# A planner for the order of one kernel's work: dense units beyond the heads' share, a fourth output tile, and banks released by their readers alone

## The reference

```
# layer "a": sparse attention; each query keeps its k_top best keys, RoPE on q and k
p = jax.nn.softmax(logits, axis=-1)
o = jnp.einsum('bhqk,bqkhd->bqhd', p, vs)            # 16 heads of 64
x = layer_norm(ALPHA * x + (o * jax.nn.silu(g)) @ w_out, ...)
# layer "b": stick-breaking attention
log_one_minus = jnp.where(before, jax.nn.log_sigmoid(-z), 0.0)
log_stick = lax.cumsum(log_one_minus, axis=3, reverse=True) - log_one_minus
a = jnp.where(before, jnp.exp(jax.nn.log_sigmoid(z) + log_stick), 0.0)
x = layer_norm(ALPHA * x + (o * jax.nn.silu(g)) @ w_out, ...)
```

## Time and profile before

| | us |
|---|---|
| median of 3 runs (1566.52 to 1567.36) | 1566.93 |
| the profiled execution | 1563.4 |
| its span, first to last instruction | 1561.6 |
| PE busy in it | 1524.5 (98%) |
| DVE, ACT, POOL busy | 1159.1, 883.7, 767.4 |
| mean granted TensorE clock | 0.995 of full |

### The profile page before, as it was taken

The page is one execution under the profiler, slowest core; times in us unless marked ns, Lnnn a source line. Parts: engine busy times, 40 slices in busy tenths (PEclk is TensorE's granted clock), DMA queues, the critical chain, the costliest instruction groups (busy, mean ns, idle before and its releaser), DMA issues.

```text
span 1561.6 us, 21827 instructions
## 1 busy us (share of the span) xinstructions
PE 1524.5 (98%) x7798; PEld 1298.5 (83%) x7798; DVE 1159.1 (74%) x2045; ACT 883.7 (57%) x1544; POOL 767.4 (49%) x745
## 2 busy tenths in 40 slices
PE   9999999999999999999999999999999999999987
PEld 7888899988788888888888788887788888888877
DVE  5999989999654688448628469976766828798876
ACT  6444788886433344234324373788884437677743
POOL 2332334434464465455545653466655336667553
PEclk9999999999999999999999999999999999999999
DMA  5988565664332232322222378755468764455551
GB/s 199 215 188 191 139 159 142 155 143 115 122 108 95 81 108 95 98 101 100 95 94 86 116 188 177 177 122 121 96 136 192 174 135 109 108 116 116 119 122 55
DMA packets 60300, 203.28 MB, mean 130 GB/s; under 512 B 6816, under 2 KB 9376, under 8 KB 60192
## 3 DMA queue, kind: packets, MB, share of 16 engines
q1 hardware_dynamic: 41184, 132.66, 25.8%
q0 software_dynamic: 19008, 69.21, 25.7%
HBM read 199.75 MB, written 2.10 MB: 129 GB/s over the span
## 4 chain that ended last, share of the span: by engine, by line
PE 84%; DVE 9%; ACT 5%; issue 1%; DMA 1%; POOL 0%; SPq 0%; ACTq 0%; DVEq 0%
PE bank L364 81%; PE bank L370 2%; DVE r L403 1%; DVE ext L403 1%; DVE r L391 1%; DVE sp_lo L391 1%; ACT soft L374 1%; DVE pt_lo L391 1%; DMA w_lo<-in_weights 0%; ACT w_hi L374 0%; DVE q_both L403 0%; DVE small L403 0%; ACT k_both L374 0%; ACT prob L374 0%; ACT ext L374 0%
## 5 line engine op out<-in xcount | busy, mean ns | idle before, releaser
L410 POOL TENSOR_TENSOR w_lo<-w_raw,w_hi 128x512 fp32r<-128x512 f32 (+1 forms) x187 | 267.8, 1454 | 254.7 <-ACT w_hi L374 254.7
L374 ACT ACTIVATE w_hi<-w_raw 128x1024 fp32r<-128x1024 f32 (+2 forms) x206 | 213.8, 1041 | 282.3 <-PE bank L364 259.8
L364 PE MATMUL bank<-x_hi,w_hi 128*128 128x512 f32 x872 | 346.9, 398 | 4.1 <-DVE q_both L403 1.7
L364 PE MATMUL bank<-x_hi,w_lo 128*128 128x512 f32 x872 | 340.7, 391 | 1.3 <-POOL w_lo L410 1.2
L364 PE MATMUL bank<-x_lo,w_hi 128*128 128x512 f32 x872 | 340.4, 390 | 0.0
L364 PEld LDWEIGHTS bank<-x_hi,w_hi 128*128 128x128 f32 x872 | 164.3, 188 | 36.7 <-ACT k_both L374 2.1
L364 PEld LDWEIGHTS bank<-x_hi,w_lo 128*128 128x128 f32 x872 | 163.8, 188 | 37.2 <-POOL w_lo L410 1.6
L364 PEld LDWEIGHTS bank<-x_lo,w_hi 128*128 128x128 f32 x872 | 164.4, 188 | 30.1
L613 POOL DMA_DIRECT2D w_lo<-in_weights x132 | 117.7, 895 | 135.0 <-ACT w_lo L374 113.8
L364 PE MATMUL bank<-a_hi,w_hi 128*128 128x512 f32 x416 | 162.0, 389 | 0.0
L364 PE MATMUL bank<-a_hi,w_lo 128*128 128x512 f32 x416 | 161.8, 389 | 0.0
(11 more groups left out here) (234 smaller groups left out, 3432.5 us busy)
## 6 DMA issues: line engine op xcount, KB each, us to landing
w_raw<-in_weights SPq DMA_DIRECT2D x223, 512.0 KB, 3.4
w_lo<-in_weights POOLq DMA_DIRECT2D x132, 512.0 KB, 6.8
alibi<-in_alibi SPq DMA_DIRECT2D x16, 256.0 KB, 4.5
w_raw<-in_weights SPq DMA_DIRECT2D x8, 384.0 KB, 3.0
r<-in_x SPq DMA_DIRECT2D x8, 256.0 KB, 6.3
r<-in_x SPq DMA_DIRECT2D x4, 512.0 KB, 6.3
out_y<-r SPq DMA_DIRECT2D x16, 128.0 KB, 1.8
w_raw<-in_weights SPq DMA_DIRECT2D x4, 256.0 KB, 5.6
```

Source lines behind the costliest of these rows:

```text
L364: return e.matmul(out, lhsT, rhs, start=start, stop=stop, skip_group_check=resumed)
L374: return self.act.run(lambda e: e.activation(out, in_, func, **kw), after, 0.07 + size(out) * 0.00086 + 0.09 * len(kw))
L410: return self.pool.run(lambda e: e.tensor_tensor(out, a, b, op), after, cost)
```

## The change

There are five edits.
- `weave`: if no stream of the heads is ripe within FAR = 1.0 us of PE's planned time, a dense unit may be filled in even beyond the share.
- `tiles`: in the heads' phase a dense tile begins only if a bank of its ring is free by plan, either at PE's planned time or at the time at which the next stream is ripe (`until`); otherwise `fill` reports "idle" and the loop goes on to the next stream.
- `stacked` returns besides its results the list of those that read the bank, and the bank is released by these alone (the two copies from `k_both` to `k_both` no longer count).
- `stick_gate`: ACT reads the bank first and releases it; DVE then takes its minimum from the copy in SBUF.
- out_b: a fourth output tile is begun in the heads' phase, after the last weighing (`last_head(1)`), on bank 4 of the ring 0 to 4; `project_and_norm` begins one tile later.

```diff
@@ -41,6 +41,7 @@
 SEAMS = (("kiwi", 0), ("qi", 0), ("vb", 0))
 FIRST_HALVED = {"out_a": 4, "out_b": 4}
 LATE_GATES = 2
+FAR = 1.0
 EXP_AND_TANH = 0
 EXP_AND_LN = 6
 
...
@@ -456,6 +459,10 @@
                 self.pe.wait(b.free)
                 return b
             self.pop()
+
+    def bank_time(self):
+
+        return min([through(b.free) for b in self.ring if not b.open and not b.pending], default=math.inf)
 
     def bank_soon(self):
 
...
@@ -640,6 +647,8 @@
 
         for key in keys:
             while key[0] in ("qa", "ka", "qb", "kb") and key[1] >= 2 and 2 * key[1] - 3 not in self.s_done:
+                yield "idle"
+            while self.in_heads and self.bank_time() > max(self.pe.time, self.until):
                 yield "idle"
             c = self.take(key)
             b = self.bank()
...
@@ -675,8 +684,8 @@
                     used[k] = [tok]
                 self.tick()
                 yield
-        for key in late:
-            while not may():
+        for n, key in enumerate(late):
+            while not may(n):
                 if self.in_heads:
                     yield "idle"
                 else:
...
@@ -885,15 +894,15 @@
         by = [scale if isinstance(scale, float) else scale[r, :] for r in own]
         func = ACT.Copy if isinstance(scale, float) else ACT.Identity
         his = [self.a_op(tiles[a][own[a], :], src[own[a], :], func, ready, scale=by[a]) for a in range(2)]
-        toks = list(his)
+        toks, reads = list(his), list(his)
         if low is not None:
             toks += [self.a_op(tiles[a][own[1 - a], :], tiles[a][own[a], :].bitcast(F32), ACT.Copy, [his[a]]) for a in range(2)]
         for a in range(2):
             yield [his[a]]
             hi = tiles[a][own[a], :]
             lo = tiles[a][own[1 - a], :] if low is None else low[a][own[a], :]
-            toks.append(self.v_stt(lo, src[own[a], :], by[a], hi.bitcast(F32), ALU.mult, ALU.subtract, ready + [his[a]]))
-        return toks
+            reads.append(self.v_stt(lo, src[own[a], :], by[a], hi.bitcast(F32), ALU.mult, ALU.subtract, ready + [his[a]]))
+        return toks + reads[2:], reads
 
     def stacked_pair(self, p, j, src, ready, scale=1.0):
 
...
@@ -1440,16 +1449,20 @@
 
 
         self.n_heads = 0
+        self.until = 0.0
         first = share = None
         waiting = [(next(s), s) for s in streams]
         while waiting:
             self.tick()
+            self.until = 0.0
             if first is not None and self.n_filled < first + int(share * self.n_heads) - slack and self.fill(1):
                 continue
             times = [self.ripe(*ask()) for ask, _ in waiting]
             n = times.index(min(times))
             if times[n] > self.pe.time:
-                if (first is None or self.n_filled < first + int(share * (self.n_heads + 1)) + (slack if ahead is None else ahead)) and self.fill(1):
+                far = times[n] > self.pe.time + FAR
+                self.until = times[n]
+                if (first is None or far or self.n_filled < first + int(share * (self.n_heads + 1)) + (slack if ahead is None else ahead)) and self.fill(1):
                     continue
                 if times[n] == math.inf:
                     if self.beside is None or self.aside() == "idle":
...
@@ -2192,10 +2205,10 @@
         g, s = self.r1[:, p, :], self.ext[1 + p % 2][:, :]
         after = [tok] + self.x_ready[(p, 1)] + ([(yield from self.know(self.gate_ready, p - 2))] if p >= 2 else [])
         yield after
-        t1 = self.v_ts(s, b.ap[:, :], -1.0, 40.0, ALU.mult, ALU.min, after)
-        yield [t1]
-        t2 = self.a_op(g, b.ap[:, :], ACT.Copy, after + [t1], scale=-1.0)
+        t2 = self.a_op(g, b.ap[:, :], ACT.Copy, after, scale=-1.0)
         b.release([t2])
+        yield [t2]
+        t1 = self.v_ts(s, g, 40.0, None, ALU.min, after=after + [t2])
         yield [t1]
         t = self.a_op(s, s, ACT.Exp, [t1])
         t = self.a_op(s, s, ACT.Ln, [t], bias=1.0)
...
@@ -2233,15 +2246,15 @@
                 yield from self.stick_gate(p, b, tok)
                 return
             j = 0 if kind == "qb" else 1
-            done[(p, j)] = yield from self.stacked_pair(p, j, b.ap, [tok], 0.125 if j == 0 else 1.0)
-            b.release(done[(p, j)])
+            done[(p, j)], reads = yield from self.stacked_pair(p, j, b.ap, [tok], 0.125 if j == 0 else 1.0)
+            b.release(reads)
             if (p, 0) in done and (p, 1) in done:
                 self.qk_ready[p] = done[(p, 0)] + done[(p, 1)]
         done = {}
 
-        def last_head():
-
-            if self.n_heads < HEADS - 1 or any(b.pending for b in self.z_banks[0]):
+        def last_head(n):
+
+            if self.n_heads < HEADS - 1 + n or any(b.pending for b in self.z_banks[0]):
                 return False
             self.ring = self.psum[0:5]
             return True
...
@@ -2249,7 +2262,7 @@
         def work():
             yield from self.tiles(stick_order(), self.h, self.hl, ready, evict)
             yield from self.two_tiles([("out_b", 0), ("out_b", 1)], lambda k: self.o_hi[:, k, :], lambda k: self.o_lo[:, k, :],
-                                      lambda k: self.got(self.os_ready, k), self.mix_evict, KT, self.os_ready, [("out_b", 2)], last_head)
+                                      lambda k: self.got(self.os_ready, k), self.mix_evict, KT, self.os_ready, [("out_b", 2), ("out_b", 3)], last_head)
         self.begin_norm()
         self.in_heads = True
         self.half_values("vb", x_ready, self.r0v)
```

22 lines of the change are left out of this document (12 added, 10 removed).

## The result

The changed kernel takes 1561.76 us (median of 8 runs, 1560.61 to 1563.82) against 1566.64 us (8 runs, 1564.52 to 1567.36): a ratio of 0.9974, 95% interval 0.9965 to 0.9983. It is faster by 4.9 us by the medians (0.31%; by the interval 0.17 to 0.35%), so no change is excluded, but it is less than half of the 12.0 us forecast and outside its range of 1550 to 1561.

What follows compares the result with a forecast made beforehand. PE, busy 1524.5 of 1561.6 us, was taken as the bound, with 19.1 us winnable from waits and slow clock. Terms 2.7 + 1.2 + 1.7 - 0.9 + 2.6 + 0.6 + 1.7 + 2.4 = 12.0 gave 1554.9 us, range 1550.0 to 1561.0.

Steps and rivals of the forecast that it cites:

- Head 4, head 8 and what comes in instead: Layer a: waits covered at head 4 (2.7 us) and head 8 (1.2, plus 1.7 slow clock), less new short waits (0.9).
- The bound from ACT's idle time: Layer a: ACT idles 4.9 of 57 us, head 4 takes 2.7, so at most 2.2 us remain for head 8.
- The clock's 1.7: Layer a, head 8: cutting the wait from 2.4 to about 1.2 us spares the slow clock, +1.7 us or 0.
- The rival that the waits only move in layer a: ACT is the bound there, heads 4 and 8 give nothing, out_b's clock still falls: gain 5.6, 1561.3 us; chance 0.25.
- The waits for a bank: Layer b: PE's waits for `q_both` (1.7 us) and `k_lo` (0.9) go, gain 2.6, at the least 1.0.
- The sums: Layer b: four sums wait for `sp_lo`, 3.0 us together; no change expected, bounds +1.5 and -1.5.
- The beginning of out_b: First unit's 2.0 us wait for `r` shrinks by 0.6 (bounds 0.2 and 2.0); slow clock behind it goes, +1.7 or 0.
- The end: Chain of 5.8 us behind the last weighing is covered by 6.8 us of units: gain 2.4, at the least 1.4.
- nothing on the path: Layer b: the gate's DVE operation saves 1.2 us of DVE time amid 31.5 us idle, so no gain is counted.
- None of the signs that the prediction gave for being wrong: `sp_lo` waits over 8 us, 2 us waits in layer a heads without any before, or PE naming POOL's `w_lo` or a DMA.
- Its low end, a gain of 6.7: Forecast's low case: both clock terms lost and layer a at its least, 12.0 - 3.4 - 0.7 - 1.2.
- The rival on POOL: Layer b: gate's new SBUF operation stalls POOL 8 x 0.54 = 4.3 us, leaving a gain of 7.7, 1559.2 us; chance 0.05.

Runs made afterwards that it cites:

- b_once2: Kernel before the change, with the second POOL operation behind each DMA issue waiting for the end of the first: 1563.73 us, ratio 0.9988.
- collide: Changed kernel with 20 trials appended, one DVE operation beside POOL trains without DMA issue: form with two SBUF inputs took 1.51 us instead of 0.69.
- u_four: Changed kernel with three output tiles of out_b in the heads' phase instead of four: 1568.92 us, ratio 1.0021 to the kernel before.
- collide2: Changed kernel with 15 trials appended, most with a DMA issue ahead of POOL's train: two-SBUF-input form took 4.53 us with the issue, 1.51 without.
- m_apart: Changed kernel, same order, but in layer b POOL waits for its own last operation before starting the next: 1554.74 us, ratio 0.9928.
- u_gate: Changed kernel with the gate's old order (DVE reads the bank, then ACT); layer b's order changes too: 1558.15 us, ratio 0.9952.

## Why the prediction failed, and where it was right

**Head 4, head 8 and what comes in instead** (+2.7, +1.2 +1.7, -0.9: 4.7) were right in sign and size: 5.45 us in the profiles' stretches, 6.4 by undoing `FAR`. The clock at 1116 us stays full. The bound from ACT's idle time was too tight: ACT was busy for 53.80 us in the same window, with more of the work done in it, and head 8's wait went nearly whole (0.2 us left, not 1.2); of the new waits one is 1.0 us. The clock's 1.7 is in part chance: before the change only one of the two waits of 2.4 us was followed by the slow clock, while in b_once2, with the same order, two such stretches stand there. The rival that the waits only move in layer a is refuted.

**The waits for a bank** (+2.6) did go, as rows: none for `q_both` or `k_lo` is left in layer b. But this step took `sp_lo`'s 1.78 us ahead of `q_both` as a given duration. In collide this form takes 0.69 us alone and 1.51 beside one operation of POOL. **The sums** held too: 3.8 us of waits for `sp_lo` instead of 3.0, within the bounds of 1.5.

**The beginning of out_b** (+0.6 +1.7) was right: the wait fell by 1.3 us, within its bounds, and the slow clock behind it went. **The end** (+2.4) was right in its mechanism. Its size was bounded by the old wait; against the new order without the fourth tile it is 7.2 us (u_four), since there the wait is 4.2 us and the clock falls behind it.

**The step that failed is what the sum puts at nothing: it has no term for the waits of layer b's weighings for `pt_lo`.** The ground for that is the sentence that DVE's operations have 31.5 us of idle time around them and are "nothing on the path". I read DVE's busy time as work, while part of it was waiting for POOL inside the operations. The changed kernel has 3.8 us of wait for a `pt_lo` that was shut out itself (held up beside POOL until its train ended), 2.1 for one behind a shut-out `sp_lo`, 0.7 for an `ext` behind the first, and two stretches of slow clock at 1.7 us each: 3.8 + 2.1 + 0.7 + 3.4 = 10.0 us. The forecast for layer b and the end was a gain of 7.3 and the stretch shows a loss of 2.1, a difference of 9.4. None of the signs that the prediction gave for being wrong tells of this: `sp_lo` stayed under 8 us, no wait of 2 us came up in layer a, and PE named neither POOL's `w_lo` nor a DMA. What went wrong came in by a wait that it didn't list.

That this was the mechanism is shown by collide2 and m_apart: the same orders with POOL's waits win 7.0 us back. That it accounts for the whole difference is not: the same remedy helps the kernel before as well, so against a kernel with the same remedy the change is worth 7.5 to 8.5 us of the 12.0. The other 3.5 to 4.5 stay open. In m_apart waits for `sp_lo`, `q_both` and `pt_lo` under 2 us each are left, which I can't put down to a single cause.

The range was too narrow by its own terms. Its low end, a gain of 6.7, takes only some of them at their least. With all at their least (2.0 for head 4, nothing for head 8 and both clock terms, -2.4, 1.0, -1.5, 0.2 and 1.4) the gain is 0.7 us, and the measured 4.9 lies above that.

The rival on POOL had the right pair of engines and the wrong size and form. The gate's operation does meet POOL, but in collide POOL loses some 0.2 us at each meeting and not 0.54, while DVE loses 0.8 (1.25 against 0.43). That u_gate won 3.6 us, near the rival's 4.3, isn't its mechanism shown, since the order changed with it. The costly meetings are those of the operations with two inputs in SBUF, which were there before the change. Of them the change made none; it only moved them to where PE had no work left.

## What to carry to other kernels

An engine's busy time can hold time in which another engine holds it up: compare the durations of one form (min, median, max) before calling an engine idle or free, and look at what ran beside the longest. A new order is priced not only by the waits that it fills, but by which operations it lays beside each other. Where GpSimd both issues DMAs and computes, and long operations of VectorE stand beside it, try one wait of GpSimd for its own last operation behind each issue (5.6 us here, 1.9 to 2.8 in the old order), or give VectorE's operations on the path one input in a bank.

## What the runs showed of the hardware that I had not expected

- Behind a DMA issue, POOL's operations start by the profile 0.3 us before the last one ends, until POOL has nothing to do (their starts are 1.01 us apart with and without it); meanwhile a DVE operation with two inputs in SBUF, or a `tensor_scalar` from SBUF to SBUF, doesn't get through: 4.53 and 4.26 us beside five operations, instead of 0.69 and 0.43. Without the issue it waits for one operation of POOL only (1.51 and 1.25).
- At one wait of POOL for its own last operation DVE gets through (0.69 and 0.43 us), and behind it POOL's operations no longer overlap.
- POOL is held up too, by some 0.4 us for each meeting with the form with two inputs in SBUF and 0.2 with the gate's (7.07 and 6.54 us instead of 6.21 for six operations).
- The forms with one input in a bank took 0.69 us in each trial.
- The part ahead of layer a's first scores, in the same order, took between 1005.8 and 1008.6 us in single executions of twelve of these kernels.
- The slow clock behind a wait isn't fixed by the wait: 6.8 and 3.4 us behind the same one of 3.8 us (u_four and the changed kernel).
